# Value stage of a decoder step: running sums carried through PSUM by ScalarE instead of added by VectorE

## The reference, cut to what matters

```python
act = jax.nn.gelu(jnp.einsum('nd,nhkd->nhk', h, u[experts]))
out = jnp.einsum('nhk,nhkd->nd', gate * act, v[experts])
y = h + out
y = rms_norm(y, norm_f_g, NORM_EPS)        # over the 2048 columns of a token
```

## Time and profile before

| What | Value |
|---|---|
| Median of three runs | 4361.43 us |
| Span of the profiled execution, first to last instruction | 4361.2 us |
| Value stage, first matmul at L2387 to last | 3189.6 to 4337.8 us |
| TensorE, share of the span | 98% |
| VectorE | 67% |
| ScalarE | 28% |

### The profile page before, as it was taken

One profiled execution on the slowest core, in us unless ns is written; L12 is line 12 of the kernel. 1 busy time (PEld: TensorE's weight loads), 2 busy tenths in 40 slices (PEclk: granted clock), 3 DMA queues, 4 the chain that ended last, 5 costly groups with the idle time before them and its releaser, 6 DMA issues.

```text
span 4361.2 us, 67488 instructions
## 1 busy us (share of the span) xinstructions
PE 4257.0 (98%) x28439; PEld 4024.2 (92%) x28439; DVE 2941.9 (67%) x4423; ACT 1218.7 (28%) x1610; POOL 742.2 (17%) x745
## 2 busy tenths in 40 slices
PE   7999999999999989999999999999999999999998
PEld 7999888998899989989999999999989999999998
DVE  3232463322334356699989999999868888888887
ACT  3221353322212121123232222222222222222234
POOL 1001002332000000000011111111122443333320
PEclk9999999999999989999999999999999999999999
DMA  6433226676343544345589999999999999999993
GB/s 195 113 102 106 85 63 196 227 244 204 110 133 116 149 104 85 78 118 131 129 243 292 292 282 297 280 292 289 278 329 356 359 338 361 364 355 356 356 344 131
DMA packets 599373, 968.32 MB, mean 222 GB/s; under 512 B 143889, under 2 KB 406033, under 8 KB 565016
## 3 DMA queue, kind: packets, MB, share of 16 engines
q1 hardware_dynamic: 508560, 519.33, 41.9%
q0 software_dynamic: 84992, 434.18, 27.0%
q10 hardware_dynamic: 5520, 10.49, 0.8%
HBM read 873.63 MB, written 85.75 MB: 220 GB/s over the span
## 4 chain that ended last, share of the span: by engine, by line
PE 94%; DVE 3%; ACT 1%; issue 1%; DMA 1%; SPq 0%; ACTq 0%; DVEq 0%
PE pair L1968 29%; PE pair L2309 28%; PE pair L2387 24%; PE quad L1968 2%; PE pair L2344 2%; PE pair L1932 1%; PE quad L2369 1%; PE quad L1932 1%; PE quad L2139 1%; ACT w_hi L890 1%; PE pair L2004 1%; PE quad L2182 1%; PE quad L2279 0%; PE quad L2054 0%; SPq L534 0%
## 5 line engine op out<-in xcount | busy, mean ns | idle before, releaser
L2309 PE MATMUL pair<-act_hi,w_hi 128*128 128x448 f32 x2048 | 757.0, 370 | 4.4 <-DVE w_lo L1648 4.4
L2309 PE MATMUL pair<-act_lo,w_hi 128*128 128x448 f32 x2048 | 748.9, 366 | 0.0
L2309 PE MATMUL pair<-act_hi,w_lo 128*128 128x448 f32 x2048 | 748.6, 366 | 0.0
L1968 PE MATMUL pair<-act_hi,w_hi 128*128 128x288 f32 x3264 | 719.0, 302 | 29.2 <-DVE act_lo L1353 12.2
L1293 DVE TENSOR_TENSOR w_lo<-w_raw,w_hi 128x2048 fp32r<-128x2048 f32 x103 | 236.2, 2293 | 746.7 <-ACT w_hi L890 746.7
L1968 PE MATMUL pair<-act_hi,w_lo 128*128 128x288 f32 x3264 | 702.6, 297 | 0.0
L1968 PE MATMUL pair<-act_lo,w_hi 128*128 128x288 f32 x3264 | 701.3, 297 | 0.0
L2387 PE MATMUL pair<-wx_hi,v_hi 128*128 128x384 f32 x2016 | 678.8, 337 | 5.5 <-DVE wx_lo L1817 3.3
L2387 PE MATMUL pair<-wx_hi,v_lo 128*128 128x384 f32 x2016 | 674.7, 335 | 0.0
L2387 PE MATMUL pair<-wx_lo,v_hi 128*128 128x384 f32 x2016 | 674.6, 335 | 0.0
L1968 PEld LDWEIGHTS pair<-act_hi,w_hi 128*128 128x128 f32 x3264 | 526.3, 190 | 67.6 <-issue 61.4
(11 more groups left out here) (339 smaller groups left out, 5467.3 us busy)
## 6 DMA issues: line engine op xcount, KB each, us to landing
w_raw<-in_peer_u_dram SPq DMA_DIRECT2D x512, 256.0 KB
v_raw<-in_peer_v_dram SPq DMA_DIRECT2D x256, 512.0 KB, 7.9
w_raw<-in_w_in_dram SPq DMA_DIRECT2D x64, 1024.0 KB
gelu_dram<-tmp SPq DMA_DIRECT2D x128, 224.0 KB, 7.5
gmat_dram<-gmat SPq DMA_DIRECT2D x48, 512.0 KB, 12.8
a_back<-gelu_dram SPq DMA_DIRECT2D x128, 192.0 KB, 6.6
g_back<-gmat_dram SPq DMA_DIRECT2D x64, 384.0 KB, 7.3
w_raw<-in_w_out_dram SPq DMA_DIRECT2D x16, 1024.0 KB
```

Of the source, the lines that this page charges most:

```text
L1968: op = m_(pair[out][:, hf, 0:TH], w[:, k, :], x[:, k, hf * TH:(hf + 1) * TH], start=(starts and k == ks[0] and i == 0), stop=(ends and k = ...
L2309: op = m_(pair[0][:, n % 2, 0:TU], w[n % 2][:, k, :], x[:, k, 0:TU], start=(k == 0 and i == 0), stop=(k == KD - 1 and i == 2))
```

## The change

ScalarE takes the running sums over from group 1 on. Ahead of tile `d` of group `g` it copies `main[:, d, 0:384]` into the bank (`seed`), TensorE adds all its matmuls onto that (no `start` flag), and behind it ScalarE copies the bank back over `main` (`take_bank`). `turn_bank(g, d)` is the pair that stands ahead of tile `d`'s other work: it takes tile d-1's bank and then seeds the same bank for tile d+3. The old semaphores `sa_tmm` and `sa_s`, both at 64 by then, count these. VectorE keeps the adds of group 0 and afterwards only waits for `acc_ps` where it had added. `value_high` and `weight_high` stand at fixed tiles of ScalarE's list now: values at 1, 3, 4, 6, 9, 11, 12, 14, weights at 2, 5, 10, 13.

```diff
-        yt_ev_d, YT = acc_done, N_VG * KD
+        yt_ev_d, YT = acc_done, KD
+        acc_out, seeded, OLD = sa_tmm, sa_s, DB * PAGES
...
+            def seed(g, d):
+
+                if g == 1:
+                    act.wait_ge(acc_done, max(d + 1, min(KD, d + 13)))
+                else:
+                    act.wait_ge(acc_out, OLD + (g - 2) * KD + d + 1)
+                if g > 1 and d < 4:
+                    act.wait_ge(acc_out, OLD + (g - 2) * KD + d + 13)
+                elif d >= 4:
+                    act.wait_ge(acc_out, OLD + (g - 1) * KD + d - 3)
+                a.copy(bank(d), main[:, d, 0:TV]).then_inc(seeded, 1)
+
+            def take_bank(g, d):
+
+                act.wait_ge(acc_ps, g * KD + d + 1)
+                a.copy(main[:, d, 0:TV], bank(d)).then_inc(acc_out, 1)
+
+            def turn_bank(g, d):
+
+                g, d = (g, d - 1) if d else (g - 1, KD - 1)
+                if g:
+                    take_bank(g, d)
+                g, d = (g, d + 4) if d < KD - 4 else (g + 1, d + 4 - KD)
+                if 0 < g < N_VG:
+                    seed(g, d)
+
+            for d in range(3):
+                seed(1, d)
             for g in range(1, N_VG):
                 after = V_GROUPS[g + 1] if g + 1 < N_VG else ()
-                for half, ns in ((1, V_GROUPS[g]), (0, after)):
-                    for n in ns[0:2]:
-                        value_high(V_AT[n, half])
-                    for n in after[0:2] if half else after[2:4]:
-                        weight_high(n)
-                    for n in ns[2:4]:
-                        value_high(V_AT[n, half])
-                if g == SP_LAST:
-                    take_expert_sums()
+                for d in range(KD):
+                    if g < N_VG - 1 or d == 0:
+                        turn_bank(g, d)
+                    half, ns = (1, V_GROUPS[g]) if d < 8 else (0, after)
+                    if d % 8 in (1, 3, 4, 6):
+                        i = (1, 3, 4, 6).index(d % 8)
+                        for n in ns[i:i + 1]:
+                            value_high(V_AT[n, half])
+                    if d % 8 in (2, 5):
+                        i = 2 * (d // 8) + (d % 8 == 5)
+                        for n in after[i:i + 1]:
+                            weight_high(n)
+                    if g == SP_LAST and d == 8:
+                        take_expert_sums()
...
             for k in range(KD):
-                act.wait_ge(acc_done, (N_VG - 1) * KD + k + 1)
+                if k < KD - 1:
+                    turn_bank(N_VG - 1, k + 1)
+                else:
+                    take_bank(N_VG - 1, k)
+                act.wait_ge(acc_out, OLD + (N_VG - 2) * KD + k + 1)
                 if k >= 2:
                     act.wait_ge(sq_summed, k - 1)
...
             for g in range(1, N_VG):
                 after = V_GROUPS[g + 1] if g + 1 < N_VG else ()
                 for d in range(KD):
-                    take_sum(g, d)
+                    dve.wait_ge(acc_ps, g * KD + d + 1)
...
-                    pe.wait_ge(acc_done, g * KD + d - 3)
+                    if g == 0:
+                        pe.wait_ge(acc_done, d - 3)
+                    else:
+                        pe.wait_ge(seeded, OLD + (g - 1) * KD + d + 1)
                     for n in ns:
-                        op = value_terms(d, n, (0, 1, 2), n == ns[0], n == ns[-1])
+                        op = value_terms(d, n, (0, 1, 2), g == 0 and n == ns[0], n == ns[-1])
                     op.then_inc(acc_ps, 1)
...
-            pe.wait_ge(acc_done, N_VG * KD)
+            pe.wait_ge(acc_out, OLD + (N_VG - 1) * KD)
```

More of the change, by code:

```diff
@@ L1827, in add_slot, with take_sum @@
                                            ALU.mult, ALU.add).then_inc(s_done, 1)
-            def take_sum(p, d):
-                dve.wait_ge(acc_ps, p * KD + d + 1)
+            def take_sum(d):
+                dve.wait_ge(acc_ps, d + 1)
                 v.tensor_add(main[:, d, 0:TV], bank(d), main[:, d, 0:TV]).then_inc(acc_done, 1)
@@ L1877, in _ @@
                     dve.wait_ge(hT_back, 32)
-                take_sum(0, d)
+                take_sum(d)
                 if d in (0, 2, 4, 8, 11):
@@ L2386, in value_terms @@
                     w, x = ((hi, xh), (hi, xl), (lo, xh))[t]
-                    op = m_(bank(d), w[:, c], x[:, :], start=(start and t == terms[0]), stop=(stop and t == terms[-1]))
+                    op = m_(bank(d), w[:, c], x[:, :], start=(start and t == terms[0]), stop=(stop and t == terms[-1]), skip_group_check=True)
                 return op
```

## The result

The changed kernel takes 4387.37 us (median of four, 4385.72 to 4389.43) against 4361.48; the ratio is 1.0058, 95% interval 1.0046 to 1.0071. The forecast was 4384. The profiled execution is the slowest of the four: its span of 4387.6 belongs to a run of 4389.43, and in every run on record the span is 1.8 us shorter than the device time, not equal to it.

The account below looks back on a forecast made before the run. TensorE is full and VectorE, though nearly full, bounds nothing. The span 4361.2 + 10.3 + 3.6 + 2.5 + 6.5 = 4384.1, with the 0.2 to the median about 4384 us; range 4371 to 4398.

Parts of the forecast that it names:

- What bounds the kernel: Value stage: TensorE full at full clock; VectorE nearly full, busy 30.4 us of 33, yet nobody's bound.
- the relief: Regular groups: 512 adds leaving VectorE, 7.5 us a group, in a time when TensorE doesn't wait: worth 0.
- The turn: ScalarE, each tile: take 0.479, gap 0.03, seed 0.465, in all 0.975 us, between 0.86 and 1.1.
- Cost 1: End of regular groups: value_high of tile 14 behind the turn delays TensorE's next group; 25 x 0.41 = 10.3 us.
- Cost 2: Group 31: ScalarE works without pause, so group 32 starts at 4307.9, not 4304.3: 3.6 us.
- The clock: Start of group 32: after TensorE idles some 5.5 us its clock falls to the 1.2 GHz level: 2.5 us.
- Cost 3: Group 32: takes and seeds queue behind ScalarE's waiting square, then its 2.22 us cycle sets the pace: 6.5 us.
- A write into PSUM: ScalarE's copies: it writes PSUM faster than SBUF, making the turn about 0.02 us shorter.
- Rival A: Group ends cost nothing, only the costs in groups 31 and 32 remain: 4374 us; chance 0.16.
- B: ScalarE late everywhere: a seed of 0.8 us makes the turn 1.3, so 4402 us; chance 0.09.
- C: No measurable change: no group-end lateness, no clock fall, half the end costs covered: 4366 us; chance 0.06.
- D: Faster: matmul steps shorten without VectorE reading PSUM beside them; 4347 us at 6 ns a step; chance 0.03.

Follow-up runs that it names:

- e6: Kernel before the change with VectorE's adds of groups 1 to 30 left out, those sums missing from its output: ratio 0.9999.
- e5: Changed kernel with ScalarE's value parts a tile ahead in groups 1 to 30 and VectorE's adds back in groups 31 and 32: ratio 1.0004.
- e10: Changed kernel with value parts, low parts and last weight_low earlier, VectorE adding again from tile 8 of group 31: ratio 1.0000.
- e1: Changed kernel with ScalarE's value parts at tiles 0, 2, 3, 5, 8, 10, 11, 13 and weights at 4, 6, 12, 14: 4373.5 us.
- e2: Changed kernel with VectorE's two weight_low of tile 14 done at tile 13, ahead of value_low; ScalarE's list untouched: 4374.6 us.
- e11: Changed kernel again, unaltered, on another chip: ratio 1.0060 to the kernel before the change on that chip.
- e3: Changed kernel with VectorE beginning to sum squares at tile 2 of the last group, not at tile 5: 4381.6 us.
- e4: Changed kernel with the change undone in groups 31 and 32 alone, where VectorE adds the banks as before: 4372.4 us.
- e7: Changed kernel with every seed copied twice, the second behind the first: ratio 1.0201.

## Why the prediction was right, step by step

- *What bounds the kernel, and that the relief is worth 0:* right. e6 measured the relief alone at 0.9999, e5 with the losses cured at 1.0004. The traces put it at 0.4 us. That group 31 held 2.8 us of waits on VectorE (0.97 and 1.87) was seen only in part; e10 got 2.2 of them back.
- *The turn, 0.975 us:* 0.98 to 0.99, with two errors that cancel. ScalarE waited 0.08 to 0.09 us for its own copy, not 0.03 (4185.48 to 4185.57), and the seed's follower starts 0.42 behind it, not 0.465.
- *Cost 1, 10.3 us:* the mechanism is shown (e1 and e2 each take one link away and all gaps go), the number of places is exact (25), and the size was 12.4. At 21 places the start is 0.44 late and restarts 0.09 slower, while I had 0.31 and 0.10; at the four behind `expert_sums` it is 0.34 and nothing, which I had not set apart. Of the missing 0.13 the hand-over from ScalarE's cast to VectorE's `value_low` makes 0.07 (4187.04 to 4187.14, 0.10 where I took 0.03); the rest is 0.01 or 0.02 each on the turn, `value_low`, `weight_low` and TensorE's undisturbed start.
- *Cost 2, 3.6 us:* 3.5. *The clock, 2.5 us:* the granted clock fell to 0.52 after 5.3 us of idling, and 18 matmuls ran at 0.32 us a step in place of 0.174: 2.6. That the size fits is partly luck: in e11, the same kernel, it was 1.3.
- *Cost 3, 6.5 us:* 8.6 less those 2.6 is 6.0. The wait for the seed of tile 7 came as forecast (2.14 us), then ScalarE's round of 2.21. e3 took away the first and kept the second. The clock fell again after that wait, at 4340, and made tile 7 last 3.7 us; it cost nothing, since none of ScalarE's takes waits for TensorE from there to the end. It did away with the 0.13 us a tile that I expected TensorE to wait behind tile 7; in e11, where the clock stayed up after the same wait, tiles 8 to 15 do start every 2.2 us, with one step of 2.5, at the pace of the seeds.
- *Two signs were wrong.* ScalarE is busy 39% and not near 50%: that was an error of arithmetic, as 512 turns of 0.975 us are 11% of the span on top of 28%. And TensorE is idle for 2.6 us ahead of the column sums, not 5:

```profile
4365.36 1.26 PE L2486 MATMUL pair<-ones,nf_sum 128*128 128x1 f32 x10 [2.60 <-ACT main L1238]
```

- *A write into PSUM:* the note that the prediction draws on stands in the Trainium skill, "ScalarE: Activation LUTs", in the section "Step-by-step: what each stage is for". The changed kernel agrees in sign: its seeds into PSUM took 484 ns and ScalarE's casts of the same size from SBUF to SBUF 508, though a copy and a cast aren't the same operation.
- *Rival A* (no cost at the group ends) is excluded by the 25 gaps, *B* (ScalarE late everywhere) by e1, in which TensorE waits for nothing in 1000 us, *C* by the ratio, *D* by e6.
- Not forecast: 1.1 us behind the column sums, all of it after the last row of VectorE, in the final stores. It belongs to the change: the stretch lasts 21.8 to 22.3 us in the seven profiles in which ScalarE carries the last group, 21.1 to 21.5 in the six in which VectorE adds there. What it comes from stays open. The 0.8 us ahead of group 1 are within what that stretch varies: on the chip of e1 to e4 group 1 began between 3209.1 and 3212.9.
- The sum is 3.4 us too small, inside its range: 2.1 too little for cost 1 and 1.9 not forecast, against 0.5 too much for cost 3.

## What to carry to other kernels

Taking work off an engine that is nearly full but that nobody waits for gained nothing here (0.4 us of 4361); ask first what the critical engine waits for, and measure the relief by leaving the work out. When a running-ahead engine gets a duty tied to the critical engine's progress, all that is behind it in its queue is tied too: price the chain from the tie to the next thing that the critical engine needs. Here one tile's move, of ScalarE's parts or of VectorE's two `weight_low` alone, gave back half of the loss.

## What the runs showed of the hardware

- ScalarE copies 128x384 floats from SBUF into PSUM in 484 ns, with its next instruction 0.42 us behind the start, and from PSUM into SBUF in 481; a copy that must wait for ScalarE's own last copy starts 0.08 us behind its end.
- A matmul that had to wait for the low weights started 0.10 us behind their end, and the next one followed after 0.25 to 0.26 us and not 0.174. ScalarE's cast to VectorE's subtraction of the same part: 0.10 us.
- After an idle time of 1.98 us of TensorE in group 32 the granted clock fell to 0.5 in the changed kernel and in e1 and stayed at 1.0 in e2 and e11. After 5.27 us it was at 0.5 both times, for 5.8 and for 2.8 us of the work that followed.
- On two of the three chips TensorE stood still in group 1 for 0.2 to 2.3 us at a time, between 3233 and 3244 us, within tile 5, in the six profiles of e5 and e7 to e11. It was not TensorE alone: in all six ScalarE and VectorE stand idle for 4 to 11 us as well, until some time between 3237 and 3244, although tiles that ScalarE had to take were done. In e6, the kernel before without adds, it was VectorE that began a `value_low` 3 us late, and TensorE waited 2.7 us for it ahead of tile 8:

```profile
3239.34 1.26 DVE L1806 TENSOR_TENSOR v_lo<-v_raw,v_hi 128x1024 fp32r<-128x1024 f32 x1 [3.12 <-PE pair L2391]
3240.66 0.44 PE L2391 MATMUL pair<-wx_hi,v_hi 128*128 128x384 f32 x1 [2.66 <-issue]
```

So kernels with and without the change have it. Its cause was not looked for.
